# Attention maxima from the high parts alone, scored in pairs on the two halves of TensorE's rows

## The reference, cut to what matters

```python
logits = jnp.einsum('bthd,bshd->bhts', qi, k).astype(jnp.float32) * ATTN_SCALE
logits = logits + (ci[..., :, None] - c_key[:, :, None, :])
logits = jnp.where(pi[:, None] >= key_pos[None, :], logits, NEG_INF)
probs = jax.nn.softmax(logits, axis=-1)
```

## Time and profile before

| | |
|---|---|
| median of 3 runs | 831.99 us (831.61 to 833.61) |
| profiled execution | 832.1 us, its span 830.3 us |
| PE busy | 799.4 us, 96% of the span |
| DVE, POOL, ACT busy | 499.4, 348.4, 315.3 us |
| chain that ended last | PE 80%, waits for nothing that is shown 6%, DVE 5%, POOL 5% |

### The profile page before, as it was taken

One profiled execution on the slowest core, in us unless ns is written; L12 is line 12 of the kernel. 1 busy time (PEld: TensorE's weight loads), 2 busy tenths in 40 slices (PEclk: granted clock), 3 DMA queues, 4 the chain that ended last, 5 costly groups with the idle time before them and its releaser, 6 DMA issues.

```text
span 830.3 us, 12914 instructions
## 1 busy us (share of the span) xinstructions
PE 799.4 (96%) x4514; PEld 646.3 (78%) x4514; DVE 499.4 (60%) x1060; ACT 315.3 (38%) x648; POOL 348.4 (42%) x292
## 2 busy tenths in 40 slices
PE   3999999999999999999999999999998999999997
PEld 3999999988878888788787865666674788878885
DVE  7944778446776867645646355777777844442222
ACT  6422241333334323333333326666777223222111
POOL 4412224454435444444344414656785344512221
PEclk9999999999999999999999999999999999999999
DMA  9342423469957346366363599999900475352221
GB/s 297 104 128 53 129 65 105 136 165 265 238 165 204 106 140 182 104 173 179 91 179 105 131 249 226 239 224 227 241 1 2 158 222 148 106 185 95 96 82 76
DMA packets 122712, 125.00 MB, mean 151 GB/s; under 512 B 30116, under 2 KB 92404, under 8 KB 122648
## 3 DMA queue, kind: packets, MB, share of 16 engines
q1 hardware_dynamic: 121208, 119.92, 54.1%
q10 hardware_dynamic: 1440, 4.26, 1.3%
HBM read 90.93 MB, written 34.92 MB: 152 GB/s over the span
## 4 chain that ended last, share of the span: by engine, by line
PE 80%; issue 6%; DVE 5%; POOL 5%; ACT 2%; DMA 1%; DVEq 0%; SPq 0%; POOLq 0%; ACTq 0%
PE PS L1877 20%; PE PS L1878 19%; PE PS L1879 19%; PE PS L2126 4%; PE PS L2127 4%; PE PS L2128 3%; POOL acc L1235 3%; PE PS L1984 2%; DVE t_val L1615 2%; PE PS L2049 1%; PE PS L2064 1%; PE PS L1899 1%; PE PS L2029 1%; POOL probs L1211 1%; ACT p_fox L1388 1%
## 5 line engine op out<-in xcount | busy, mean ns | idle before, releaser
L1166 POOL TENSOR_TENSOR ops<-s_sum,ops 128x512 fp32r<-128x512 f32 x64 | 87.5, 1377 | 111.2 <-ACT ops L1264 111.2
L1877 PE MATMUL PS<-t_hi,ops 128*128 128x512 f32 x256 | 101.1, 395 | 0.0
L1878 PE MATMUL PS<-t_lo,ops 128*128 128x512 f32 x256 | 99.8, 390 | 0.0
L1879 PE MATMUL PS<-t_hi,ops 128*128 128x512 f32 x256 | 99.8, 390 | 0.0
L1166 POOL TENSOR_TENSOR ops<-raw,ops 128x512 fp32r<-128x512 f32 x48 | 65.5, 1365 | 69.0 <-ACT ops L1264 68.8
L1187 POOL TENSOR_TENSOR w_plain<-raw,w_plain 128x1024 fp32r<-128x1024 f32 x10 | 28.0, 2800 | 84.4 <-ACT w_plain L1293 84.4
L1694 DVE TENSOR_TENSOR z_tmp<-u,PS 128x512 f32<-128x512 f32 x48 | 33.0, 687 | 49.1 <-PE PS L1879 28.2
L1235 POOL TENSOR_TENSOR acc<-acc,p_fox 128x400 f32<-128x400 f32 (+5 forms) x76 | 59.9, 808 | 5.0 <-ACT p_fox L1388 4.0
L1264 ACT ACTIVATE ops<-s_sum 128x512 fp32r<-128x512 f32 x64 | 39.6, 623 | 52.8 <-DVE s_sum L1496 41.8
L1388 ACT ACTIVATE p_fox<-PS,neg_c_col 128x512 f32<-128x512 f32 (+5 forms) x112 | 54.3, 536 | 13.7 <-PE PS L2035 9.1
L1879 PEld LDWEIGHTS PS<-t_hi,ops 128*128 128x128 f32 x256 | 48.1, 188 | 10.6
(11 more groups left out here) (206 smaller groups left out, 2182.9 us busy)
## 6 DMA issues: line engine op xcount, KB each, us to landing
raw<-in_w_in_dram SPq DMA_DIRECT2D x34, 512.0 KB, 5.2
q_dram<-stage_b SPq DMA_DIRECT2D x32, 256.0 KB, 3.0
g_dram<-stage_b SPq DMA_DIRECT2D x32, 256.0 KB, 2.1
tanh_g<-g_dram SPq DMA_DIRECT2D x16, 512.0 KB, 4.1
max_k<-k_dram SPq DMA_DIRECT2D x16, 260.0 KB, 5.5
max_c<-neg_c_dram SPq DMA_DIRECT2D x8, 520.0 KB, 6.4
x_all<-in_x_dram SPq DMA_DIRECT2D x8, 512.0 KB, 7.7
raw<-in_w_in_dram SPq DMA_DIRECT2D x16, 256.0 KB, 4.7
```

The source lines that it names most:

```text
L1166: nc.gpsimd.tensor_tensor(ops[:, i % OPS, 1], op_source(p, name), ops[:, i % OPS, 0].bitcast(F32), ALU.subtract).then_inc(op_ready, 1)
L1877: pe.matmul(dst, hi_w, hi, start=first, stop=False)
L1878: pe.matmul(dst, hi_w, lo, start=False, stop=False)
L1879: return pe.matmul(dst, lo_w, hi, start=False, stop=last)
```

## The change

Both halves of `max_k` now hold the high key parts, and a piece is q_hi·k_hi over 64 contraction rows: even pieces on partitions 0 to 63, odd ones on 64 to 127. The two matmuls of a pair stand next to each other, and the masks, still over all 128 rows, come behind both. TensorE waits once ahead of the pair, until DVE has reduced both pieces of the pair before. Each of the two PSUM banks has a semaphore of its own for "scored".

```diff
-        max_scored = sem("max_scored")
+        max_scored = sems("max_scored", 2)
@@ load_maxima
                 if head:
-                    sp.wait_ge(max_scored, n_maxima // HEADS * head)
+                    for x in range(2):
+                        sp.wait_ge(max_scored[x], n_maxima // HEADS * head // 2)
...
-                for x, part in enumerate((Q0, Q1)):
-                    sp.dma_start(max_k[part].bitcast(F32), kd[1 + j, x][half]).then_inc(max_loaded, 16)
+                for part in (Q0, Q1):
+                    sp.dma_start(max_k[part].bitcast(F32), kd[1 + j, 0][half]).then_inc(max_loaded, 16)
@@ DVE, reduce_maxima
-                    dve.wait_ge(max_scored, n + 1)
+                    dve.wait_ge(max_scored[n % 2], n // 2 + 1)
@@ TensorE, behind product i
-                for st in maxima.get(i, []):
+                pieces = maxima.get(i, [])
+                for y, st in enumerate(pieces):
...
-                    if n >= MAX_RING:
-                        pe.wait_ge(max_reduced, n - MAX_RING + 1)
-                    bank = PS[:, MAX_BANK + n % MAX_RING, :]
-                    ins = pe.matmul(bank[:, 0:w], max_q[:, t * P:(t + 1) * P], max_k[:, c0:c0 + w], start=True,
-                                    stop=not st["last"])
+                    if n >= MAX_RING and not y:
+                        pe.wait_ge(max_reduced, n - MAX_RING + len(pieces))
+                    part = (Q0, Q1)[n % 2]
+                    ins = pe.matmul(PS[:, MAX_BANK + n % MAX_RING, 0:w], max_q[part, t * P:(t + 1) * P],
+                                    max_k[part, c0:c0 + w], start=True, stop=not st["last"])
+                    if not st["last"]:
+                        ins.then_inc(max_scored[n % 2], 1)
+                for st in pieces:
                     if st["last"]:
-                        ins = pe.matmul(bank[:, w - P:w], ident_b, causal, start=False, stop=True)
-                    ins.then_inc(max_scored, 1)
+                        w = st["w"]
+                        pe.matmul(PS[:, MAX_BANK + st["n"] % MAX_RING, w - P:w], ident_b, causal, start=False,
+                                  stop=True).then_inc(max_scored[st["n"] % 2], 1)
```

More of the change, by code:

```diff
@@ L1066, in _ @@
                         sp.wait_ge(max_reduced, n_maxima)
-                        sp.wait_ge(max_scored, n_maxima)
+                        for x in range(2):
+                            sp.wait_ge(max_scored[x], n_maxima // 2)
                         sp.wait_ge(windows_stored, 16 * 8)
```

## The result

Five runs of the changed kernel have a median of 841.05 us (839.49 to 842.74), five of the kernel before 832.27 (831.61 to 833.61). The ratio is 1.0105, with a 95% interval of 1.0089 to 1.012. The forecast was 840.2, in a range of 826 to 848.

The account below looks back on a forecast made before the run. The prediction took TensorE's (PE's) own matmul stream to bound the stage. Pair terms of 0.67 us and w/2400 made a head 5.85 us against 4.83, +8.2 us over 8 heads: 831.99 + 8.2 = 840.2 us, range 826 to 848.

Parts of the forecast that it names:

- What bounds: From 195 to 450 us TensorE's own matmuls bound the stage; a nanosecond in its stream moves the end 1 to 1.
- Term 1: Going from 128 rows into the 64-row halves, the stream stops: 0.09 us per pair, bounds 0 and 0.09.
- the three places: Trace rows changing height, 128 to 8, back, and 16 to 80; each was read as costing 0.09 us.
- Rival A: Changing to 64 rows needs no stop and both weights load ahead: 824 us, or 828 us; chance 0.22.
- Terms 2 to 4: Pair to mask: 0.10 unhidden weights, w/2400 and 0.01 streaming side by side, 0.09 and 0.01 back, 0.01 mask weights.
- Term 2: The pair's first weights aren't loaded ahead: 0.10 us for both halves together, bounds 0 and 0.10.
- rival C: The second half's weights load behind the first's, starting the second piece 0.10 late: 844.6 us; chance 0.13.
- Rival B: The stops are there, but weights load ahead across them: +2.0, 834 us; chance 0.07.
- Term 5: From the last mask's start to the second product matmul behind the pair: 0.36 us; a second mask adds 0.06.
- the sum: Per pair 0.67 us and w/2400; per head 5.85 us against 4.83, +8.2 us for 8 heads.
- The rest at nothing: DMAs, TensorE's single wait for both pieces, DVE's reductions and the clock were all costed at nothing.

Follow-up runs that it names:

- The small matmuls over 64 and 32 rows: One 16-column matmul over 64 or 32 contraction rows added ahead of each pair in the order-alone kernel: 856.14 and 855.24 us, against 840.15 over 128 rows.
- order-alone kernel: The changed kernel with score matmuls over all 128 rows again and the low key parts back: 833.34 us, ratio 1.0002 to the kernel before.

## Why the prediction was right

*What bounds.* PE without a gap, 1 to 1. The stretch that holds all pairs grew by 8.1 us and the median by 8.8. The view of waits has no wait of PE in the stage, before or after.

*Term 1, the stop on the way in:* forecast 0.09, measured 0.32 - 0.23 = 0.09, in all kinds of pair. The small matmuls over 64 and 32 rows agree. But the rows that the price came from were weaker than the prediction had them. The 8-row matmuls are fp32 (`ident` and `neg_c_rows`) and stand between fp32r ones, so two of the three places change the type as well as the height. A change to fp32 with 64 output rows, at full height, stops the stream by the same 0.09 (209.77 - 209.45 - 0.23). Only the third place, from 16 rows to 80, is fp32 on both sides. That two places of three could not tell height from type did no harm here, and this is luck. Nor does every change of height stop the stream. The trace of the kernel before also goes from 80 rows to 128, fp32 with 64 output rows on both sides:

```profile
509.49 0.39 PE L2079 MATMUL PS<-p_t,v_a 80*64 80x128 f32 x4
509.71 0.39 PE L2079 MATMUL PS<-p_t,v_b 128*64 128x128 f32 x4
```

The second row starts 0.17 ahead of the end of the first, as in an ordinary stream. So heights of 80 and 128 follow each other freely here, where 64 and 32 beside 128, and 16 beside 80, don't. Rival A's remark that the only changes of height in the trace go to 32 rows or fewer passed over these. Where between 64 and 80 rows the border lies, no run shows.

*Terms 2 to 4:* forecast from pair to mask for (384, 400): 0.10 + 0.17 + 0.01 + 0.10 = 0.38, measured 0.39. Term 2 had a doubt, whether the second half's weights come behind the first's (rival C). The two loads span 0.19, as one does, so C is out. Rival B needs loads ahead of the pair, and there the loader is idle 56 times. Rival A needs both.

*Term 5:* forecast 0.37 with the mask's own load, measured 0.35. So the mask's load, 0.01 in the sum, can't be seen, and 0.01 more was rounding.

*Per pair* the sum had 0.84, 0.78, 0.84, 0.88 and 0.83 for (144, 272), (256, 272), (384, 400), (512, 272) and (384, 384), against 0.82, 0.77, 0.83, 0.88 and 0.82. That is 0.01 too much in most pairs. Added up over all 56, each from the product matmul ahead of it to the second one behind it, the pairs take 51.3 us before and 59.0 after: 7.7 more, where 8.2 was forecast. The other 1.2 us of the span isn't in the sum. Of it, 0.4 lies in the products between the pairs, 0.2 ahead of the first pair and 0.6 behind the last. No part of the change was meant to reach there, and the kernels of the last section move by more than that without a cause in the code. So the forecast lands within 0.9 us of the median by two small misses in opposite directions, and the second of them isn't settled.

*The rest at nothing:* the order-alone kernel has the new semaphores, the single wait and the order, and stands at 1.0002. The DMA part was shown by no run of its own, but nothing waits for it in the changed kernel either.

The Trainium skill's rule ("TensorEngine Tiling (Array Packing)", section "Key Properties"), that a change of the tiling mode drains TensorE, agrees with these runs for heights of 64 and 32: 0.29 us there and back. It doesn't hold for every change of the tile. A matmul of 128x64 between those of 128x128 costs nothing more in fp32r (stages 260.0 and 260.1), so for that change the measurement decides. Whether the chip counts it as a change of mode, the trace doesn't show.

## What to carry to other kernels

Two short matmuls on the two row halves of TensorE save the narrower one's stream, at most 0.21 us for 512 columns, an estimate from the 2.4 GHz level. One visit to the halves between full-height matmuls costs 0.29 us with a mask behind the pair, and about 0.4 straight back to a product. So a single pair per visit can't pay in a stream that TensorE bounds. Behind a mask, an estimate: with 0.18 saved by a pair of (384, 384) two such pairs in a row would pay, and with the mean of 0.12 to 0.14 here three. Without the mask two pairs of (384, 384) would fall just short. None of this was tried, and it needs more PSUM banks than the two that are free. What did pay was to leave work out. The kernel before without its 64 masks takes 827.05 us, faster than both, and the softmax stays the same function, since the number subtracted cancels; it only grows by what later keys of the diagonal block add. For which inputs it would grow so far that the exponentials become too small, no run here shows.

## What else the runs showed of the hardware

**Type and width.** A 128x64 tile in fp32 stops the stream (0.32 to the small matmul, 1.36 to the second product matmul), in fp32r it doesn't (0.23 and 1.05). Part of the 1.36 is the second pass that fp32 takes here (x2 in its row). The stop that the attention's column halves show before their fp32 matmuls is thus no sign for tiles in fp32r.

**The clock at the change of stage.** Outside the maxima the kernels differ by some us that no edit explains. The stretch view of the kernel before and of the order-alone kernel (length, busy times, granted clock third from the end):

```profile
504.00:508.00 4.00, 3.85 (x14) 2.97 (x16) 0.44 (x4) 3.80 (x9) 2.22 (x6) 0.57 0.51 152
```

```profile
494.00:498.00 4.00, 3.94 (x14) 1.38 (x12) 0.00 (x0) 2.34 (x4) 2.11 (x3) 0.57 1.14 231
...
508.00:512.00 4.00, 3.93 (x12) 2.23 (x14) 1.03 (x6) 2.97 (x8) 0.96 (x3) 0.57 1.04 263
```

Where the attention begins TensorE has waits, and behind them the granted clock falls from 2.4 to 1.2 GHz for a while: once in the one kernel's profile, twice in the other's. The order-alone kernel's span is 834.1 us and not 830.3, though its stage is 0.2 shorter. Over its 12 runs the time goes loosely with the mean granted clock: 831.27 and 831.68 us at 0.999, 835.41 at 0.992, but also 832.89 at 0.993 and 833.36 at 0.998. So the clock is a likely part of the cause, and it isn't shown to be all of it. The kernel before without masks has two such stretches there too and one more near 20 us, at a mean of 0.993 in its profile; that is where I look for the part of its miss that isn't in the stage, though no experiment was made of it.
